# Token sums first, down chunks split in halves and earlier, and load slots in turn, in a kernel of two networks

## What is computed

```
def swiglu_2(x, w_gate_up, w_down):
    g, u = jnp.split(x @ w_gate_up, 2, axis=-1)
    return (jax.nn.silu(g) * u) @ w_down

for i in range(DEPTH):                                   # DEPTH = 2
    h = h + FFN_RES_SCALE * swiglu_2(rms_norm(h, ffa_norm[i]), ffa_w_gate_up[i], ffa_w_down[i])   # a0, a1
    hn = rms_norm(h, mix_norm[i])
    h = h + (even_mixer if i % 2 == 0 else odd_mixer)(hn, ...)
    h = h + FFN_RES_SCALE * swiglu_2(rms_norm(h, ffb_norm[i]), ffb_w_gate_up[i], ffb_w_down[i])   # b0, b1
    gate = jax.nn.sigmoid(rms_norm(h, ple_norm[i]) @ ple_w_gate[i])
    h = h + gate * (p[i] @ ple_w_proj[i])
```

## Time and profile before

| | us |
|---|---|
| median of 3 runs | 4040.25 (4037.43 to 4048.16) |
| profiled execution | 4053.44, span 4051.6 |
| TensorE busy | 3875.3 (96%) |
| VectorE busy | 2535.8 (63%) |
| ScalarE busy | 1547.7 (38%) |
| GpSimd busy | 569.6 (14%) |
| mean granted TensorE clock | 0.974 of full speed |

### The profile page before, as it was taken

How to read it: one execution, slowest core, us unless ns; L and a number is a source line. 1 busy time by engine, 2 the same in 40 slices (tenths; PEclk the granted TensorE clock), 3 DMA queues, 4 the chain that set the end, 5 groups by cost and what they waited for, 6 DMA issues and landing times.

```text
span 4051.6 us, 54907 instructions
## 1 busy us (share of the span) xinstructions
PE 3875.3 (96%) x22330; PEld 3312.1 (82%) x22330; DVE 2535.8 (63%) x3687; ACT 1547.7 (38%) x2344; POOL 569.6 (14%) x604
## 2 busy tenths in 40 slices
PE   7999999999999989999899989999999999999998
PEld 5788988788878778887799867899789988778986
DVE  5646555656559985335677655777676764566775
ACT  3335443322233233223344454444444443344443
POOL 0025551100013220003000143000100010010001
PEclk9999989999999999999999999999999999999999
DMA  6220002546231113233344311444244433014442
GB/s 203 86 75 1 1 1 94 166 128 196 77 103 49 59 53 126 93 96 102 90 133 136 97 63 57 107 134 121 98 133 128 125 105 95 22 58 130 120 138 71
DMA packets 275285, 392.10 MB, mean 97 GB/s; under 512 B 10843, under 2 KB 249243, under 8 KB 263516
## 3 DMA queue, kind: packets, MB, share of 16 engines
q1 hardware_dynamic: 263804, 347.70, 25.9%
q0 software_dynamic: 11232, 40.90, 5.6%
HBM read 345.31 MB, written 2.10 MB: 86 GB/s over the span
## 4 chain that ended last, share of the span: by engine, by line
PE 66%; DVE 15%; ACT 4%; issue 3%; POOL 0%; DVEq 0%; ACTq 0%
PE ps L482 12%; PE ps L484 12%; PE ps L483 12%; PE ps L2535 6%; PE ps L2537 6%; PE ps L2536 6%; DVE wlo L462 3%; ACT whi L438 2%; PE ps L1679 2%; PE ps L4081 1%; PE ps L4068 1%; DVE h L843 1%; PE ps L4051 1%; DVE dtmp L841 1%; PE ps L489 1%
## 5 line engine op out<-in xcount | busy, mean ns | idle before, releaser
L462 DVE TENSOR_TENSOR wlo<-raw,whi 128x1024 fp32r<-128x1024 f32 (+4 forms) x461 | 726.6, 1581 | 622.2 <-ACT whi L438 622.0
L438 ACT ACTIVATE whi<-raw 128x1024 fp32r<-128x1024 f32 (+4 forms) x461 | 609.3, 1326 | 970.7 <-PE ps L484 708.3
L482 PE MATMUL ps<-X,whi 128*128 128x512 f32 x1384 | 551.8, 399 | 14.5 <-DVE wlo L462 9.4
L483 PE MATMUL ps<-X,whi 128*128 128x512 f32 x1384 | 542.9, 392 | 0.0
L484 PE MATMUL ps<-X,wlo 128*128 128x512 f32 x1384 | 542.7, 392 | 0.0
L2535 PE MATMUL ps<-TT,whi 128*128 128x256 f32 x1248 | 357.8, 287 | 25.2 <-ACT E L2597 11.6
L2536 PE MATMUL ps<-TT,whi 128*128 128x256 f32 x1248 | 356.1, 285 | 0.0
L2537 PE MATMUL ps<-TT,wlo 128*128 128x256 f32 x1248 | 356.0, 285 | 0.0
L482 PEld LDWEIGHTS ps<-X,whi 128*128 128x128 f32 x1384 | 262.4, 190 | 79.1 <-issue 24.2
L482 PE MATMUL ps<-SDh,whi 128*128 128x512 f32 x704 | 281.9, 400 | 33.8 <-DVE wlo L462 15.1
L484 PEld LDWEIGHTS ps<-X,wlo 128*128 128x128 f32 x1384 | 262.3, 190 | 56.2
(11 more groups left out here) (628 smaller groups left out, 8285.4 us busy)
## 6 DMA issues: line engine op xcount, KB each, us to landing
raw<-in_ffn_w SPq DMA_DIRECT2D x44, 1024.0 KB, 5.4
raw<-in_gu_a SPq DMA_DIRECT2D x44, 1024.0 KB, 4.8
raw<-in_gu_b SPq DMA_DIRECT2D x44, 1024.0 KB, 4.9
raw<-raw POOLq DMA_DIRECT2D x78, 512.0 KB, 4.6
mslot<-in_mod_w SPq DMA_DIRECT2D x28, 1024.0 KB, 8.1
raw<-in_mod_w SPq DMA_DIRECT2D x20, 1024.0 KB, 5.9
raw<-in_ffa_w_down SPq DMA_DIRECT2D x24, 768.0 KB, 4.5
raw<-in_ffb_w_down SPq DMA_DIRECT2D x24, 768.0 KB, 4.6
```

The lines of the kernel that those rows point to most:

```text
L438: act.activation(k.target(k.whi, u), k.source(u), ACT.Copy).then_inc(*k.ev.put("act_whi", ("hi", n)))
L462: dve.tensor_tensor(k.target(k.wlo, u), k.source(u), k.target(k.whi, u).bitcast(F32), ALU.subtract).then_inc(*k.ev.put("dve_wlo", ("lo", n ...
L482: pe.matmul(o, wh, xh, start=first, stop=False)
L483: pe.matmul(o, wh, xl, start=False, stop=False)
```

## The change

Slots are taken in turn from the first chunk on. The four token sums stand first in an FFN, ahead of the splits and the norm, and GpSimd's norm of the first network waits for them; its matmul stands before a0's first down chunk, and each tile of h is multiplied just before its residual. In the plain chunks the splits stand at other places between scaling, silu and product. In a column chunk by seven products, scaling, silu and product of the first half come to its end, and the tail has two steps instead of three. The first down chunk of each part is split in two halves, and TensorE multiplies the first half for both banks, then the other tiles in turns of the banks. The splits behind down chunk cc stand behind its first residual (in part 3, on ScalarE, behind the first gained tile). `ple_in` and `ple_up` move to the chunks 0 and 1.

```diff
@@ -147,3 +147,3 @@
         self.list.append(c)
-        c.slot = min(range(NR + (wide is not None)), key=lambda i: (self.loaded[i] is not None and self.loaded[i], i))
+        c.slot = min(range(NR + (wide is not None)), key=lambda i: (-1 if self.loaded[i] is None else self.loaded[i], i))
         c.before, self.loaded[c.slot] = self.loaded[c.slot], c.j
@@ -248,2 +248,4 @@
                       wide=wide if part < len(S_PARTS) - 1 else None)
+                if cc == 0:
+                    W[(st, "d", part, 0)].half = nch * 256
 
@@ -437,3 +439,6 @@
         act.wait_ge(*k.ev.at(("used", u.before)))
-    act.activation(k.target(k.whi, u), k.source(u), ACT.Copy).then_inc(*k.ev.put("act_whi", ("hi", n)))
+    to, src, half = k.target(k.whi, u), k.source(u), u.c.half or 0
+    if half:
+        act.activation(to[:, 0:half], src[:, 0:half], ACT.Copy).then_inc(*k.ev.put("act_whi", ("hi half", n)))
+    act.activation(to[:, half:], src[:, half:], ACT.Copy).then_inc(*k.ev.put("act_whi", ("hi", n)))
 
@@ -460,4 +465,9 @@
     u = k.W.split[n]
+    to, src, hi, half = k.target(k.wlo, u), k.source(u), k.target(k.whi, u).bitcast(F32), u.c.half or 0
+    if half:
+        dve.wait_ge(*k.ev.at(("hi half", n)))
+        dve.tensor_tensor(to[:, 0:half], src[:, 0:half], hi[:, 0:half], ALU.subtract).then_inc(
+            *k.ev.put("dve_wlo", ("lo half", n)))
     dve.wait_ge(*k.ev.at(("hi", n)))
-    dve.tensor_tensor(k.target(k.wlo, u), k.source(u), k.target(k.whi, u).bitcast(F32), ALU.subtract).then_inc(
+    dve.tensor_tensor(to[:, half:], src[:, half:], hi[:, half:], ALU.subtract).then_inc(
         *k.ev.put("dve_wlo", ("lo", n), *([("raw free", u.c.j)] if u.piece in (None, 6) else [("raw free", u.c.j - 1)] if u.piece == 5 else [])))
@@ -810,2 +820,3 @@
     pool.wait_ge(*ev.at(("sqsum", "n5", 7)))
+    pool.wait_ge(*ev.at(("T", "a0", 3)))
     for m in range(8):
@@ -826,10 +837,8 @@
 
-def own_norm_dve(k, dve):
+def own_norm_dve(k, dve, i):
 
-    rstd_dve(k, dve, "n4", k.sq[0][:, :])
-    for i in range(8):
-        if i == 0:
-            dve.wait_ge(*k.ev.at(("rstd", "n4")))
-        dve.scalar_tensor_tensor(k.h[:, i, :], k.h[:, i, :], k.col("fin1", i), k.sq[0][:, :], ALU.mult, ALU.mult).then_inc(
-            *k.ev.put("dve_h"))
+    if i == 0:
+        dve.wait_ge(*k.ev.at(("rstd", "n4")))
+    dve.scalar_tensor_tensor(k.h[:, i, :], k.h[:, i, :], k.col("fin1", i), k.sq[0][:, :], ALU.mult, ALU.mult).then_inc(
+        *k.ev.put("dve_h"))
 
@@ -2565,4 +2574,4 @@
                     gained_sum_pe(k, pe, norm)
-            if (norm, c) == ("n5", 1):
-                own_norm_pe(k, pe)
+        if (st, part) == ("a0", 0):
+            own_norm_pe(k, pe)
         nt = 2 * nch
@@ -2573,6 +2582,9 @@
                 room(k, pe, (st, "d", part, cc * 2 + s))
-            pe.wait_ge(*ev.at(("lo", w.n)))
-            early = nt - 2 if cc == 0 else 0
-            for s, m in [(s, m) for s in range(2) for m in range(early)] + [(s, m) for s in range(2) for m in range(early, nt)]:
+            pe.wait_ge(*ev.at(("lo" if cc else "lo half", w.n)))
+            order = [(s, m) for s in range(2) for m in range(nt)] if cc else (
+                [(s, m) for s in range(2) for m in range(nch)] + [(s, m) for m in range(nch, nt) for s in range(2)])
+            for s, m in order:
                 o = slice(s * 128, s * 128 + 128)
+                if cc == 0 and (s, m) == (0, nch):
+                    pe.wait_ge(*ev.at(("lo", w.n)))
                 if cc == 0 and s == 0:
@@ -2618,7 +2630,5 @@
         s_keep_act(k, act, st, c, 6, k.E[c % 2][:, 1, :, 0:256])
-        s_silu_act(k, act, st, c, 0)
-    if at == 1:
-        s_silu_act(k, act, st, c, 1)
         s_high_act(k, act, st, part, 2 * (c - c0), k.E[c % 2][:, 0, 0, :])
-    if at == 2:
+        s_silu_act(k, act, st, c, 1)
+    if at == 1:
         s_high_act(k, act, st, part, 2 * (c - c0) + 1, k.E[c % 2][:, 1, 0, :])
@@ -2641,3 +2651,3 @@
             s_keep_act(k, act, st, c, kept, (e[:, 0, :, 0:256], e[:, 1, :, 256:512], e[:, 0, :, 256:512])[i - 1])
-        if tail and i < 3:
+        if tail and i < 2:
             s_tail_act(k, act, st, c - 1, i)
@@ -2646,2 +2656,3 @@
                 split_hi(k, act, n)
+    s_silu_act(k, act, st, c, 0)
 
@@ -2657,4 +2668,2 @@
         for c in range(c0, c0 + nch):
-            if (norm, c) == ("n5", 2):
-                std_act(k, act, "n4", 7, k.psum[NB], k.sq[0][:, :])
             if c >= S_FFNS[st]:
@@ -2666,4 +2675,4 @@
             if c == 0:
-                t_act(k, act, st, 0)
-                t_act(k, act, st, 1)
+                for kk in range(4):
+                    t_act(k, act, st, kk)
             next_hi(k, act, (st, "g", c))
@@ -2671,3 +2680,4 @@
                 h_norm_act(k, act, norm)
-                t_act(k, act, st, 2)
+            behind = k.W.follows(k.W[(st, "u", c)].n)
+            split_hi(k, act, behind[0])
             for s in range(2):
@@ -2676,7 +2686,5 @@
                 act.activation(ft, ft, ACT.Silu).then_inc(*ev.put("act_ffn", ("silu", st, part, 2 * c + s)))
-                if c == 0 and s == 0:
-                    t_act(k, act, st, 3)
+            for n in behind[1:]:
+                split_hi(k, act, n)
             for s in range(2):
-                if s:
-                    next_hi(k, act, (st, "u", c))
                 s_high_act(k, act, st, part, 2 * c + s, k.E[0][:, s, c, :])
@@ -2685,11 +2693,9 @@
         s_tail_act(k, act, st, c, 1)
-        s_tail_act(k, act, st, c, 2)
         for n in s_freed(k, st, c, 6):
             split_hi(k, act, n)
+        if (st, part) == ("a0", 0):
+            std_act(k, act, "n4", 7, k.psum[NB], k.sq[0][:, :])
         for cc in range(4):
-            if cc:
-                next_hi(k, act, (st, "d", part, cc - 1))
-            if (st[0], part, cc) == ("b", 3, 1):
-                ple_in_act(k, act, li)
-                ple_up_act(k, act, li)
+            if (st[0], part) == ("b", 3) and cc < 2:
+                (ple_in_act, ple_up_act)[cc](k, act, li)
             if (st, part, cc) == ("a1", 3, 1):
@@ -2697,5 +2703,6 @@
             if part == 3:
-                for m in (cc * 2, cc * 2 + 1):
-                    gained_act(k, act, tag, m)
-        next_hi(k, act, (st, "d", part, 3))
+                gained_act(k, act, tag, cc * 2)
+            next_hi(k, act, (st, "d", part, cc))
+            if part == 3:
+                gained_act(k, act, tag, cc * 2 + 1)
 
@@ -2762,8 +2769,6 @@
     if at == 0:
-        s_glu_dve(k, dve, st, c, 0)
         s_scaled_dve(k, dve, st, c, 1, [("kept", st, c, "C21"), ("C22", st, c)])
-    if at == 1:
         s_low_dve(k, dve, st, part, m, e[:, 0, 0, :])
         s_glu_dve(k, dve, st, c, 1)
-    if at == 2:
+    if at == 1:
         s_low_dve(k, dve, st, part, m + 1, e[:, 1, 0, :])
@@ -2782,2 +2787,3 @@
             s_add_dve(k, dve, st, c, "C12", "Z", 5, 4, e[:, 0, :, 256:512])
+            s_scaled_dve(k, dve, st, c, 0, [("C11", st, c), ("C12", st, c)])
         if i > 0:
@@ -2785,6 +2791,5 @@
                 split_lo(k, dve, n)
-        if tail and i < 3:
+        if tail and i < 2:
             s_tail_dve(k, dve, st, c - 1, i)
-        if i == 6:
-            s_scaled_dve(k, dve, st, c, 0, [("C11", st, c), ("C12", st, c)])
+    s_glu_dve(k, dve, st, c, 0)
 
@@ -2802,6 +2807,7 @@
             if c == 0:
-                t_dve(k, dve, st, norm, 0)
-                t_dve(k, dve, st, norm, 1)
-                t_low_dve(k, dve, st, 0)
-                t_low_dve(k, dve, st, 1)
+                for kk in range(4):
+                    t_dve(k, dve, st, norm, kk)
+                    if kk % 2:
+                        t_low_dve(k, dve, st, kk - 1)
+                        t_low_dve(k, dve, st, kk)
             next_lo(k, dve, (st, "g", c))
@@ -2809,5 +2815,4 @@
                 h_norm_dve(k, dve, norm)
-                t_dve(k, dve, st, norm, 2)
-                t_dve(k, dve, st, norm, 3)
                 dve.wait_ge(*ev.at(("rstd", norm)))
+            behind = k.W.follows(k.W[(st, "u", c)].n)
             for s in range(2):
@@ -2816,13 +2821,12 @@
                     *ev.put("dve_ffn", ("gr", st, part, 2 * c + s), ("out", st, "g", c, s)))
-                if c == 0:
-                    t_low_dve(k, dve, st, 2 + s)
+            split_lo(k, dve, behind[0])
             for s in range(2):
-                buf = k.E[0][:, s, c, :]
-                if s:
-                    next_lo(k, dve, (st, "u", c))
                 dve.wait_ge(*ev.at(("mm", st, "u", c, s)))
                 dve.wait_ge(*ev.at(("silu", st, part, 2 * c + s)))
-                dve.tensor_tensor(buf, buf, k.bk.of((st, "u", c, s))[:, :], ALU.mult).then_inc(
+                dve.tensor_tensor(k.E[0][:, s, c, :], k.E[0][:, s, c, :], k.bk.of((st, "u", c, s))[:, :], ALU.mult).then_inc(
                     *ev.put("dve_ffn", ("glu", st, part, 2 * c + s), ("out", st, "u", c, s)))
-                s_low_dve(k, dve, st, part, 2 * c + s, buf)
+            for n in behind[1:]:
```

(18 more changed lines are left out.)

4 lines of the change are left out of this document (2 added, 2 removed).

## The result

The kernel after takes 3989.4 us (median, 3987.2 to 3993.5), before 4042.0 beside it: ratio 0.987 [0.9855, 0.9886], 52.6 us less. The forecast was 3978 in a range of 3958 to 4010: the direction and the range held, the gain was sized 10 us too high. The terms that it was added up from missed by more, and in part cancelled.

The account below looks back on a forecast made before the run. TensorE, busy 96% of the span, was taken as the bound, so the question was which idle time could go. Terms summing to 62.5 us, taken off the median 4040.25, gave 3978 us, range 3958 to 4010.

Parts of the forecast that it names:

- Start: Start of the kernel: three loads go out at once, leaving one stop of about 1.3; 7.0 us gained, bounds 5 to 8.3.
- Head of a0: Beginning of FFN a0: GpSimd's norm waits for the token sums, shortening TensorE's stops; 12.0 us gained, bounds 6 to 14.
- First seams: FFN first seams: norms before their own residuals, splits ready earlier; 9.5 us gained in a0, 2.9 in the other three.
- surcharge of 0.27 a stop: At TensorE's stops: a stop shown as x costs about x + 0.27 us.
- Second, third and fourth seams: Seams: split halves gain 11.5 us at second and fourth; earlier tails and four tile rows gain 14.0 at third.
- rival (2): At eight seams the kept product, not the split, holds TensorE, so halves bring nothing: 3989.5 us; chance 0.12.
- Heads of b0, a1, b1: Beginnings of these FFNs: first token sum to fourth product takes 28.6 instead of 32.0 us; 10.5 gained in all.
- Rival (3): The heads only reshuffle and the start's loads crowd: 3990.5 us; chance 0.12.
- Ends: FFN ends: 1.9 and 4.4 us gained in a0 and a1, 5.6 lost each in b0 and b1; -4.9 in all.
- Rival (1): The ends spread: part 3's chain is late, 16 chunks lose about 1 us each: 3994 us; chance 0.12.
- Rival (4): Slower than before: the wait before the second residual stalls TensorE at all 64 down chunks, 96 us: 4074; chance 0.04.
- Rival (5): Low clock stays where stops shrink, about 9 us: 3987; no separate chance, counted in the forecast's own range 3965 to 3992.

Follow-up runs that it names:

- the slots alone: Kernel before with one line changed: load slots taken in turn from the first chunk on; 4037.2 us against 4043.6, ratio 0.9973.
- The kernel with the DMA in the norm: Kernel after, but in a0 GpSimd issues the accumulating DMA for the first pair's weight sum in the middle of its norm; 3979.4 us, ratio 0.9841.
- halves-off kernel: Kernel after, but each part's first down chunk is split in one piece again on both engines; 4000.6 us, ratio 0.9887.
- after again: Kernel after, unchanged, measured once more; 3992.2 us against 4042.5 for before, ratio 0.9867.

## Why the prediction was nearly right, point by point

**Start:** 8.07 against 7.0. The loads go out and come in earlier as forecast, but the stops were the wrong thing to add up. In before and in after a load ends the last wait of the start, and from there to the first helper matmul both take the same time; so the gain is how much earlier that load is in, 22.02 instead of 30.09. How long TensorE stops for it says little: 1.15 with the slots alone and 2.29 in after, with the same 22.02, because the matmuls ahead took 13.42 in the one and 12.30 in the other.

**Head of a0:** 8.10 against 12.0, and 0.9 of the 8.10 is the stop of 0.76 that was forecast with the seam. So nearly 5 us are missing, the largest single miss. The first two stops are 0.45, where 1.0 was forecast, and none. The step that failed is "the third falls from 1.66 to some 1.1": I moved GpSimd's norm behind the sums and weighed only what it slows beside it, not what stands behind it in GpSimd's own list. 3.32 came, and 2.9 us of low clock behind it. The kernel with the DMA in the norm has neither; its head gains 12.96, or 12.0 without the 0.9, which is the forecast. So the whole miss is the queue. By the Trainium skill's rule I had put the head at 10, with both first stops at 1 us. VectorE was slowed as the rule has it: in after the split at 1920.05 takes 2.03 and the one at 1925.44 takes 2.22, while a split of that shape takes 1.23 at 1936.99. But the stops were 0.45 and none, so this cost the head nothing that can be seen.

**First seams:** 7.97, or 8.9 with the stop of 0.76, against 9.5, and 3.13 against 2.9. In a0 all four stops went, and the stretch of low clock too. The row behind the stop of 4.97 in before, and the whole seam in after (columns as in the earlier trace rows):

```profile
2001.50:2007.00 5.50, 5.49 (x17) 4.45 (x18) 4.40 (x5) 0.00 (x0) 0.00 (x0) 0.69 0.53 191
```
```profile
1956.46:1989.52 33.06, 33.06 (x146) 27.19 (x145) 27.68 (x31) 10.65 (x11) 0.86 (x1) 1.00 0.44 143
```

Too large was the surcharge of 0.27 a stop: 7.97 less 5.91 of stops and 1.7 of clock leaves 0.36 for three. At the stops of 0.76 it is 0.16, by the halves-off kernel.

**Second, third and fourth seams:** 10.9 against 11.5, and 14.01 against 14.0. That the split and not the kept product held TensorE was decided by one sum, 2679.12 + 1.76 against 2681.14, and the halves-off kernel bears it out, so rival (2) falls. The third seams' sum is right by luck: at full clock a seam gained 2.7 (25.08 to 22.35), with the pairs behind it 2.9, and not 3.1. The stops of 0.45 and 0.3 that I left there came as 0.09 and none, but the surcharges that I added weren't there. And of the low clock both stretches went, not one, which is 1.4 us more. (For a second or fourth seam the terms listed sum to 1.48, not 1.44.)

**Heads of b0, a1, b1:** 14.38 against 10.5. In b0, from the first token sum to the fourth product it takes 2510.42 - 2481.99 = 28.4 us, the 28.6 of the forecast; before 32.0. The mis-sized term is "little of the low clock saved": the head gained 4.8, so 4.8 - 3.6 = 1.2 us was clock (granted 0.83 from 2551.5 to 2560 in before, 1.00 behind the last stop in after). In a1 the clock was more of it: its stops fell by 1.9, the head by 4.7. Rival (3) falls.

**Ends:** a0 0.5 against 1.9 (a stop of 2.16 before the mixer, on the last tile, which two blocks per tile did not cover), a1 3.2 against 4.4 (once 4.4 us of the mixer's clock are taken off), b0 and b1 15.9 lost against 11.2. The mechanism and the place are as forecast: 2.43 and 5.96 stand for 1.7 and 7.0. The mis-sized term is "1.3 of small ones", which came to 3.3 in b0: at the gate's start TensorE waits 1.68 for a split that can't begin before the third down chunk is used up, and 1.64 at tile 5. In b1 the stop at the gate's start is 0.09, but the 10 us before it ran at a granted clock of 0.85, and 1.6 us of its 8.9 are lost behind the gate's first chunk, in code that stands as before. Rival (1), a chain that is late at all 16 chunks, did not happen; a0's and b's ends are its only trace.

**Rival (4)**, all 64 chunks stalled, did not come: putting the split back behind both residuals changed 1.1 us at the 48 chunks of the parts 0 to 2. **Rival (5)** asked whether the low clock stays. It went at more places than I had counted (a0's first seam, the two third seams that had it, b0's head), and came at new ones behind the new stops: 2.9 us in a0's head, 2 at b0's gate.

Taken together the missed terms sum to 8 us (62.5 against 54.3). In the table a0's head and the ends fell short by 11, and the start and the other heads gave 5 more than forecast: so the total is nearer than its terms, and that is luck. The two large misses are of the same kind: work moved ahead of something that I had not listed.

## What to carry to other kernels

When an instruction is moved or made to wait on an in-order engine, write down everything behind it in that engine's list, DMA issues above all, before pricing the move. A rule "next split behind the first residual" can be nearly idle at 48 chunks and cost 8.6 us at b0's end, where the next stage's matmuls wait for the last tiles; give it to the places one by one, or let the consumer take two blocks a tile. Where a load ends the last wait of a stretch, the gain is the difference of the two arrivals and not of the stops. For edits of a few us compare distances between the same two matmuls of two traces, and first look how much those distances vary where nothing was changed.

## What the chip showed that I had not expected

TensorE's clock makes executions of one and the same kernel differ by more than most parts of this change. The four runs of after again gave 3994.7, 3992.1, 3992.3 and 3975.4 us, with a mean granted clock of 0.977, 0.978, 0.979 and 0.982; the eight of the slot kernel 4023.5 to 4048.0, with 0.979 at the lowest time and 0.974 at the highest. The instructions are the same, and before a0, where the traces differ most, TensorE is idle for 57.4 to 58.2 us in all three windows shown above: no stop explains their 15 us. By the Trainium skill ("TensorE: Matmul & The Clock Gate", "What's actually happening") the gate runs on its own phase, so that the number of slow matmuls changes from run to run. The traces agree for the stretch before a0; at other places the low clock came back at the same instructions each time, as in a1's mixer in before and with the slots alone. The spread in a kernel of 4 ms is 19 and 24 us here, 0.5 or 0.6%, more than the largest term of the forecast. What decides it was not tried.

A releaser can be named wrongly where several waits stand before one instruction: 0.76 us was put down to ScalarE's kept product in before and in the kernel without halves, and left with the split's halves in both directions.
